# Probabilities normalised and gated before their transposition, instead of factors for the outputs

## The reference, cut to what matters

```python
def masked_softmax(logits, valid, sink=None):
    ...
    e = jnp.exp(logits - m)
    den = jnp.sum(e, axis=-1, keepdims=True)
    if sink is not None:
        den = den + jnp.exp(sink - m)
    return e / jnp.where(den > 0, den, 1.0)

def gqa_attend(q, k, v, dist, valid, table, sink=None):
    ...
    p = masked_softmax(logits, valid, sink)
    return jnp.einsum('ngrql,nlgd->nqgrd', p.astype(v.dtype), v)

def a_finish(x, o, z, gate, w_out):
    return x + gate * ((o.reshape(n, t, HD) * jax.nn.silu(z)) @ w_out)
```

## Time and profile before

| | us |
|---|---|
| runs | 1702.78, 1703.77, 1699.12 |
| median | 1702.78 |
| profiled execution: span | 1699.8 |
| TensorE busy / weight loads | 1588.0 / 1425.7 |
| VectorE busy | 934.7 |
| ACT busy | 613.7 |
| POOL busy | 485.8 |
| layer A, pairs 0 to 6 / last | 118 to 410 / 410 to 454 |
| layer B, pair 0 / 1 to 6 / last | 754 to 862 / 862 to 1498 / 1498 to 1582 |

### The profile page before, as it was taken

One profiled execution on the slowest core, in us unless ns is written; L12 is line 12 of the kernel. 1 busy time (PEld: TensorE's weight loads), 2 busy tenths in 40 slices (PEclk: granted clock), 3 DMA queues, 4 the chain that ended last, 5 costly groups with the idle time before them and its releaser, 6 DMA issues.

```text
span 1699.8 us, 31847 instructions
## 1 busy us (share of the span) xinstructions
PE 1588.0 (93%) x11936; PEld 1425.7 (84%) x11936; DVE 934.7 (55%) x2396; ACT 613.7 (36%) x1356; POOL 485.8 (29%) x294
## 2 busy tenths in 40 slices
PE   4579999999699997899999999999999999998997
PEld 1478888888599997788998989989899898886897
DVE  3635555555645415555555755657556575578556
ACT  3413333333214414224434344344443444444112
POOL 0232412221841315355121121211212112149661
PEclk9689999999799997999999999999999999999999
DMA  9233333232612134501021130211101111033732
GB/s 329 92 92 106 106 106 106 107 106 88 236 67 75 47 136 124 141 26 35 15 64 35 29 84 17 88 35 29 35 17 38 35 29 35 18 84 104 255 145 100
DMA packets 82594, 145.16 MB, mean 85 GB/s; under 512 B 19170, under 2 KB 54146, under 8 KB 82274
## 3 DMA queue, kind: packets, MB, share of 16 engines
q1 hardware_dynamic: 69210, 128.64, 23.1%
q10 hardware_dynamic: 10288, 8.46, 1.6%
q0 software_dynamic: 2944, 6.04, 1.3%
HBM read 128.96 MB, written 19.35 MB: 87 GB/s over the span
## 4 chain that ended last, share of the span: by engine, by line
PE 86%; DVE 4%; DMA 3%; ACT 3%; issue 2%; SPq 2%; ACTq 0%; DVEq 0%
PE PS L1032 15%; PE PS L1034 15%; PE PS L1033 15%; PE PS L1287 11%; PE PS L1300 10%; PE PS L1267 5%; PE PS L1268 4%; PE PS L1406 2%; PE PS L1277 2%; DMA WR<-w_ada 2%; PE PS L1229 1%; DMA WR<-sw_v 1%; PE PS L1296 1%; PE PS L1249 1%; PE PS L1382 1%
## 5 line engine op out<-in xcount | busy, mean ns | idle before, releaser
L1032 PE MATMUL PS<-HT_r,WR_r 128*128 128x344 f32 x1344 | 448.8, 334 | 20.0 <-DVE XT_r L1823 15.3
L1034 PE MATMUL PS<-HT_r,WR_r 128*128 128x344 f32 x1344 | 433.4, 322 | 0.0
L1033 PE MATMUL PS<-XT_r,WR_r 128*128 128x344 f32 x1344 | 433.2, 322 | 0.0
L669 POOL TENSOR_TENSOR WR_r<-WR,ONE 128x1024 fp32r<-128x1024 f32 x60 | 116.6, 1943 | 1042.6 <-DMA WR<-w_b 598.3
L1631 ACT ACTIVATE PB<-PB,NM 128x257 f32<-128x257 f32 (+9 forms) x384 | 248.8, 650 | 171.4 <-DVE NM L2023 171.1
L1032 PEld LDWEIGHTS PS<-HT_r,WR_r 128*128 128x128 f32 x1344 | 257.2, 191 | 22.9 <-issue 19.9
L1033 PEld LDWEIGHTS PS<-XT_r,WR_r 128*128 128x128 f32 x1344 | 257.1, 191 | 0.0
L1034 PEld LDWEIGHTS PS<-HT_r,WR_r 128*128 128x128 f32 x1344 | 256.5, 191 | 0.0
L2036 DVE COPY PT<-PS 128x256 f32<-128x256 f32 (+2 forms) x192 | 121.6, 633 | 211.8 <-PE PS L1287 210.7
L1287 PE MATMUL PS<-CST,PB 128*128 128x128 f32 (+1 forms) x1360 | 226.5, 286 | 0.9 <-ACT PT L1639 0.9
L1300 PE MATMUL PS<-PT,VT 128*64 128x128 f32 x2592 | 204.0, 285 | 6.0 <-DVE PT L2036 2.8
(11 more groups left out here) (310 smaller groups left out, 2389.5 us busy)
## 6 DMA issues: line engine op xcount, KB each, us to landing
WR<-w_ada SPq DMA_DIRECT2D x64, 512.0 KB, 5.4
WR<-w_b SPq DMA_DIRECT2D x32, 512.0 KB, 3.3
WR<-w_a SPq DMA_DIRECT2D x17, 512.0 KB, 4.4
STR<-scratch SPq DMA_DIRECT2D x128, 48.0 KB, 1.9
XT<-x SPq DMA_DIRECT2D x8, 516.0 KB, 9.1
HT<-x SPq DMA_DIRECT2D x8, 516.0 KB, 7.2
HT<-x_mid SPq DMA_DIRECT2D x8, 516.0 KB, 5.0
STR<-scratch SPq DMA_DIRECT2D x128, 32.0 KB, 1.9
```

The source lines that it names most:

```text
L669: pool.tensor_tensor(high_r, raw, ONE[:, 0:1].unsqueeze(2).to_broadcast([P, NC, P]), ALU.mult).then_inc(sem("w_split"), 1)
L1032: pe.matmul(out, hw[:, k, :], high, start=(k == 0), stop=False)
L1033: pe.matmul(out, hw[:, k, :], low, start=False, stop=False)
L1034: return pe.matmul(out, lw[:, k, :], high, start=False, stop=(k == NC - 1))
```

## The change

Steps rg, t1 and the transposes of kind "o" are gone. A new step "nr" stands once per unit: VectorE takes the reciprocals of the unit's row sums (two columns) and multiplies the untransposed probabilities in PB by reciprocal and gate, in place, one instruction per head (1.0 for the gate in layer A); cmp's is one 128 x 512 product with spread factors. TensorE's transposes of PB wait for it (semaphore "nr") where they waited for "ex". In oe the output in bank 6 is multiplied by 0.5 and by SZ. In the plan nr of the next unit stands after the eviction of the present unit's second group (of its first where it has one), cmp's after sm of sel0. Banks 4 and 5 now hold only groups of probabilities; waits elsewhere for t1 are waits for oe.

```diff
@@ phase_plan
+    if phase == "a":
+        emit("nr", units[0])
...
-    pending, late = [], None
+    pending = []
...
     def flush():
-        if late:
-            emit("tr", late)
-            emit("t1", late)
         for g in pending:
             emit("pv", g)
...
+            if un["b"] == "cmp":
+                emit("nr", un)
...
-        late = None
-        for hf in ending[0:1] if un["b"] != "cmp" else []:
-            emit("rg", hf)
         emit("tr", gs[0])
         emit("ev", gs[0])
...
+        normalise = nxt is not None and not to_cmp
+        if normalise and len(gs) == 1:
+            emit("nr", nxt)
         for a, g in enumerate(gs[1:]):
             emit("tr", g)
             emit("ev", g)
+            if normalise and a == 0:
+                emit("nr", nxt)
...
@@ TensorE
-                        if x["kind"] == "o":
-                            pe.wait_ge(sem(ph + "_rg"), x["h"] + 1)
-                            for i in range(QB // 2):
-                                last = pe.transpose(PS[:, bank, i * P:(i + 1) * P], SS[:, i * P:(i + 1) * P], ident)
-                        else:
-                            un = x["unit"]
-                            pe.wait_ge(sem(ph + "_ex"), un["parts"][-1]["x"] + 1)
...
+                        un = x["unit"]
+                        pe.wait_ge(sem(ph + "_nr"), un["i"] + 1)
...
@@ VectorE
-                    elif what == "rg":
...
+                    elif what == "nr":
+                        un, b = x, x["b"]
                         dve.wait_ge(sem(ph + "_ex"), un["parts"][-1]["x"] + 1)
...
+                        if b == "cmp":
...
+                            step(dve.tensor_reduce(RG[:, :, :], p4, AX, ALU.add))
+                            step(dve.tensor_scalar(RG[:, :, :], RG[:, :, :], 1.0 / BIG, None, ALU.max))
+                            step(dve.reciprocal(RG[:, :, :], RG[:, :, :]))
+                            step(dve.tensor_tensor(RG[:, :, :], RG[:, :, :], SG[:, :, c0:c0 + 2], ALU.mult))
+                            dve.tensor_tensor(p4, p4, RG[:, :, :].unsqueeze(3).to_broadcast([P, QB, 2, NCB]), ALU.mult)\
+                               .then_inc(sem(ph + "_nr"), 1)
                         else:
...
+                            step(dve.reciprocal(RG[:, 0, :], DEN[:, BR[b], :, un["qb"]]))
+                            for s in range(2):
+                                p_ = PB[:, un["slot"] + s, un["at"]:un["at"] + un["keys"]]
+                                gate = 1.0 if ph == "a" else SG[:, un["qb"], c0 + s:c0 + s + 1]
+                                ins = dve.tensor_scalar(p_, p_, RG[:, 0, s:s + 1], gate, ALU.mult, ALU.mult)
+                            ins.then_inc(sem(ph + "_nr"), 1)
-                    elif what == "t1":
...
-                        dve.wait_ge(sem(ph + "_t1"), h + 1)
+                        dve.wait_ge(sem("fill_ev"), gate_done(ph, b, it, half))
...
-                            dve.tensor_tensor(out, PS[:, 6, :], SS[:, :], ALU.mult).then_inc(sem(ph + "_oe"), 1)
+                            dve.scalar_tensor_tensor(out, PS[:, 6, :], 0.5, SZ[b][:, cols], ALU.mult, ALU.mult).then_inc(sem(ph + "_oe"), 1)
```

More of the change, by code:

```diff
@@ L204, in phase_plan @@
         gs = un["groups"]
-        ending = [g["ends"] for g in gs if g["ends"]]
         here = slots.get((it, j), [])
@@ L259, in phase_plan @@
             emit("ex", nxt["parts"][0])
[L260 to L265, removed]
         if un["b"] != "cmp" and not to_cmp:
@@ L381, in build @@
         DEN = sb("DEN", [P, 3, 2, QB])
-        RG = sb("RG", [P, QB // 2, 2])
+        RG = sb("RG", [P, QB, 2])
         NSK = sb("NSK", [P, H + 1])
@@ L766, in _ @@
                 split_output("b", c)
[L767 removed]
+            pool.wait_ge(sem("b_mix"), 4 * (PAIRS - 1))
             split_output("b", NC - 2)
@@ L897, in _ @@
             bring_back(4, 6)
-            sp.wait_ge(sem("a_t1"), plans["a"]["HF"])
+            sp.wait_ge(sem("a_oe"), plans["a"]["HF"])
             sp.wait_ge(sem("szs_set"), PAIRS)
@@ L1273, in pairs @@
                         bank = 4 + x["n"] % 2
[L1274 to L1287 removed]
+                        un = x["unit"]
+                        pe.wait_ge(sem(ph + "_nr"), un["i"] + 1)
+                        for i, item in enumerate(x["items"]):
+                            if un["b"] == "cmp":
+                                n, src = 2 * NCB, PB[:, un["slot"], un["at"] + item * 2 * NCB:un["at"] + (item + 1) * 2 * NCB]
+                            else:
+                                kb, s = item
+                                n, src = P, PB[:, un["slot"] + s, un["at"] + kb * P:un["at"] + (kb + 1) * P]
+                            last = pe.transpose(PS[0:n, bank, i * P:(i + 1) * P], src, ident)
                         last.then_inc(sem(ph + "_tr"), 1)
@@ L1910, in add_mask @@
                     step(dve.tensor_tensor(m, m, CST[:, C_FAR:C_FAR + P], ALU.add))
-                def free_sums(h, it, b):
-                    if h:
-                        dve.wait_ge(sem(ph + "_oe"), h)
-                    adds = 0 if ph == "a" else len([x for x in pl["halves"] if "add" in x and x["h"] < h])
-                    if adds:
-                        dve.wait_ge(sem("b_mix"), adds)
                 if ph == "a":
@@ L2036, in pairs @@
                         dve.tensor_copy(PT[0:m, c % 2, 0:n], PS[0:m, 4 + x["n"] % 2, 0:n]).then_inc(sem(ph + "_evd"), 1)
-                    elif what == "rg":
-                        it, b, half, h = x["it"], x["b"], x["half"], x["h"]
-                        un = [u for u in pl["units"] if u["it"] == it and u["b"] == b and u["qb"] in (None, 4 * half + 3)][0]
+                    elif what == "nr":
+                        un, b = x, x["b"]
                         dve.wait_ge(sem(ph + "_ex"), un["parts"][-1]["x"] + 1)
-                        den = DEN[:, BR[b], :, :].rearrange("p s q -> p q s")
-                        if b == "cmp" and half == 0:
+                        c0 = BR[b] * H + 2 * un["it"]
+                        if b == "cmp":
@@ L2043, in pairs @@
                             p4 = PB[:, un["slot"], un["at"]:un["at"] + un["keys"]].rearrange("p (q s c) -> p q s c", q=QB, s=2)
-                            step(dve.tensor_reduce(den, p4, AX, ALU.add))
-                            step(dve.tensor_scalar(den, den, 1.0 / BIG, None, ALU.max))
-                        rg = RG[:, :, :]
-                        step(dve.reciprocal(rg, den[:, 4 * half:4 * half + 4, :]))
-                        free_sums(h, it, b)
-                        wide = rg.unsqueeze(3).to_broadcast([P, QB // 2, 2, HDIM])
@@ L2066, in pairs @@
                         last = [g for u in pl["units"] if u["it"] == it and u["b"] == b for g in u["groups"] if g["ends"] is x][0]
-                        out = MT[:, it, 512 * half:512 * half + 512]
+                        cols = slice(512 * half, 512 * half + 512)
+                        out = MT[:, it, cols]
                         dve.wait_ge(sem(ph + "_pv"), last["c"] + 1)
-                        dve.wait_ge(sem(ph + "_t1"), h + 1)
+                        dve.wait_ge(sem("fill_ev"), gate_done(ph, b, it, half))
                         if b in ("a", "cmp"):
```

39 lines of the change are left out of this document (6 added, 33 removed).

## The result

The changed kernel takes 1733.34 us in the median of four runs, against 1701.74 for the kernel before: 1.0201 times, 95% interval 1.0174 to 1.0227. It is 31.6 us slower. The forecast was 14 us slower, to 1717, with a range of 1683 to 1745: the direction and the place in the range hold, the size is off by more than a factor of two.

What follows compares the result with a forecast made beforehand. TensorE was taken as the bound, except in the last pairs, where it waits for chains between engines. Lateness 50.9 - 39.9 freed + 3 for the clock = +14 us, giving 1717 us; range 1683 to 1745.

Steps and rivals of the forecast that it cites:

- pairs 1 to 6 only 3.7 in all: Layer B's middle pairs: lateness of 3.7 us in all, as POOL is mostly idle and filling work covers.
- nothing is charged: Compressed unit's step, 8 times: replaces factors that TensorE waited for anyway, so no cost was counted.
- The walk: Every unit: from ACT's last sum through reciprocal, POOL waits and multiplications to lateness at the first transpose; sum 50.9 us.
- The price of a multiplication: New multiplications on VectorE: 0.30 us for 256 keys, 0.43 for 512, 0.71 for 1024, without waits.
- What bounds the kernel, and the two kinds of stage: TensorE bounds layer B's pairs 1 to 6, gaining about 15 us; in last pairs it waits for chains between engines.
- 33.4 + 6.5 = 39.9 us: TensorE, whole kernel: 33.4 us of factor transposes and 6.5 us of idle time before them go.
- POOL's waits decide: Units beside busy POOL: both VectorE multiplications wait for POOL instructions; total lateness 50.9 us, or 8.7 without such waits.
- Layer A's last pair (13.0 late): Layer A's last pair: blocks 2 to 6 come 2.5, 4.6, 1.4, 2.8 and 1.8 us late, 13.0 in all.
- Clock, +3: Layer B's last pair: a lower granted clock costs between 0 and 10.5 us, taken as 3.
- one wait a unit: Rival, all units: only one of two multiplications waits for POOL; 25.6 us late, total 1689 us; chance 0.17.
- no waits at all: Rival, all units: multiplications never wait for POOL; 8.7 us late, total 1672 us; chance 0.07.
- the third: Rival, layer B's pairs 1 to 6: VectorE bounds in a ring, 102 units 0.5 us late, 1768 us; chance 0.08.

Runs made afterwards that it cites:

- Four pieces: Changed kernel with POOL's splits of weights and outputs cut into four instructions of 256 columns each: 1699.89 us, 0.9992 times the kernel before.
- a form that does not wait: Changed kernel, POOL's instructions whole, with multiplications that also reduce into an accumulator (gate not applied in layer B as in the kernel): 1747.90 us.
- pieces of four and eight: Changed kernel with POOL's splits cut into four instructions of 256 columns, 1699.89 us, or into eight of 128 columns, 1705.90 us.

## Why the prediction was wrong

- **"pairs 1 to 6 only 3.7 in all" and "nothing is charged" for the compressed unit:** the step that failed. The new step costs 21.6 us there, by stage. TensorE waits 6.8 us at the compressed units, which were charged nothing, and 8.6 us at sel1, win1, win3 and win5; some 3.4 us more are the two stretches at half clock. Four pieces take away 9.8 of the 21.6, about as much as the compressed units' waits and the clock's fall make together. The walk asked at every unit whether its own multiplications meet POOL, but not what the instructions ahead of them in VectorE's queue wait for (L1975 and L2046 above).
- **The price of a multiplication:** 0.30 us for 256 keys and 0.71 for 1024 were taken from one row with two column factors. In layer B they take 0.41 and 0.81 without a wait, so about 0.1 us more each. Where the prediction found units late by hundredths, TensorE waits 0.25 to 0.60 us at four of each pair's; that is the 8.6 us in the list of waits, and it stays with pieces (8.2).
- **What bounds the kernel, and the two kinds of stage:** right in part. The transposes that go are worth most where TensorE is full (16.4 us in the middle pairs), and nearly nothing in B's last pair. But the change as a whole lost in every stage, the middle pairs included.
- **"33.4 + 6.5 = 39.9 us" freed:** mis-sized, 32. Stretches from load to load over-count in the middle pairs (19.1 against 16.4), and in B's last pair other waits for POOL took the place of those removed (0.2 of 5).
- **POOL's waits decide, and both multiplications can wait:** the mechanism was right, its share smaller than forecast. The sum put 42 of its 50.9 us on these waits (50.9 less the 8.7 without them); when only the length of POOL's instructions was changed, 33 of the 64 us went, and a form that does not wait shows no waits. Against the multiplications of the same shape that meet no POOL instruction, one or both are over 0.1 us longer in 47 of the 192 units: both in 15 (layer A, B's last pair, and one unit of B's pair 0), one in 32, among them all 18 of pairs 1 to 6. So the rule "the second waits for the whole next one" holds at a third of them; at sel2 of pair 3 the two take 2.41 and 0.47 us. These waits sum to 87 us on VectorE, which is most of why its busy time rose by 181 us instead of 105; only a part of them reaches TensorE.
- **Layer A's last pair (13.0 late):** over-sized, 7.8 for the stretch up to layer B. Blocks 4 and 6 have one wait of 0.25 us each instead of two.
- **Clock, +3:** not measured by itself. In B's last pair the same matmuls are busy 69.7 us at a clock of 0.85, against 64.9 at 0.91 without the step, and part of that fills idle time; the pair's whole price, 19.1, is within a microsecond of 17.1 + 3. The clock's fall in the middle pairs was not foreseen.
- **Rivals:** one wait a unit is the commoner case among the units that wait, but at 15 of them both multiplications do; no waits at all is refuted. The sign that was named for the third, TensorE idle before transposes in pairs 1 to 6, came: 15.4 us over 102 units, 0.15 us a unit, which is the size that the prediction gave as eating the whole gain there. It is not a ring in which every unit comes late, though: 30 units wait, and VectorE is busy 456 of 641 us. The third's condition for eating the gain was thus met by another way.

In sum: some 8 us less freed than forecast, most of it in B's last pair and the middle pairs, and some 10 us more paid: 18 more in the middle pairs, 3 more in each of layer A's first pairs and B's pair 0, and 5 less in layer A's last pair (by stage, where the profiled executions lie 76 us apart and not 64). The direction of the total came out as forecast, that of the middle pairs did not. What is open is how the 57 us of the multiplications divide exactly into waiting for POOL and length: pieces of four and eight take away more waits but make POOL slower, and a run without POOL's splits was not made.

## What to carry to other kernels

A step that is put between a producer and a consumer which wait for each other costs what its length exceeds the slack by, and so the slack has to be listed unit by unit, together with what stands ahead of the step in its engine's queue. Where GpSimd works beside VectorE's SBUF instructions, look at the length of one GpSimd instruction and not at its busy share: cutting it in four gave 33 us to one kernel and 8 to the other, and cutting it in eight cost the first 6 us again. An idle engine (ACT, 36% busy) is no refuge when the evictions stand in its queue.

## What the runs showed of the hardware

- A VectorE multiplication over 256 keys takes 0.355 us with one column factor and an immediate, and 0.41 with two columns; in the form with an accumulator it takes 0.48 and 0.54.
- VectorE instructions of 16 and 14 columns, which take 0.17 and 0.23 us when nothing is in their way, took up to 1.8 us in the kernel before and up to 2.3 us in the run without the new step when they met POOL's splits of 1024 columns. The reciprocals of two columns take 145 to 170 ns at all 192 places. The multiplications with an accumulator differ by at most 10 ns within one shape, beside POOL's splits or not.
- POOL's splits of 1024, 256 and 128 columns take 1.99, 0.68 and 0.44 us (multiplication): a quarter of the work costs a third of the time, an eighth more than a fifth.
